# A two-part transformer kernel: its state-space layer's tables by closed form, its angles on GpSimd, its corrections on VectorE

## The chip, the cores and the metric

The kernel runs on one core of one Trainium2 chip. The metric is the device time of one launch, in microseconds (us). TensorE is called PE, VectorE DVE, ScalarE ACT, GpSimd POOL and SyncE SP, as in the profile; SP issues all transfers.

## What is computed

Two blocks of two layers each over 512 tokens of width 1024: a diagonal state-space layer (S5), sliding-window attention, MLPs, then a second block with a Mamba-2 layer and differential attention. Only the S5 layer, which comes first, is touched. For 64 groups of 16 channels with 64 complex states each:

```
dt = exp(log_dt);  a = exp(lam_re*dt) * (cos(lam_im*dt) + i sin(lam_im*dt))
coef = (a - 1) / lam;  bb = coef * b
x[t] = a * x[t-1] + bb @ u[t];   y[t] = Re(c @ x[t]) + d * u[t],  u = rmsnorm(h) * gain
mix = A * sigmoid(G),  (A, G) = gelu(y) @ w_glu
```

## The kernel before

**Tiling.** Tokens are cut into 64 steps of 8 (STEP), the groups into 8 blocks of 8 (GB). Within a step the recurrence is a small matrix product; from step to step it is a scan with the eighth power of a. The complex rotation is taken out of the scan, so that it has a real factor: the step sums are multiplied with cos and sin of angles (psi times the step's index) ahead of it and turned back behind it.

**The start.** s5_loads (L378) issues all loads on SP in one row: par, h, const, B, C, the first inputs Ur, then four units of weights. s5_vector (L492) forms dt's products, reduces the angle (L510), gets mag, sin and cos of one power from ACT (L430 to L433), and builds all powers of a by repeated complex products cmul (L546, six linked instructions each, eight calls, L564 to L572): TA for the outputs, PB for the inputs. Then signs (L593 to L595), the diagonal DI (L597), the first input tables (L600) and the step-wise norm factor ru (L603 to L606). link waits for each instruction before the next. Meanwhile ACT squares h in eight tiles through two buffers (L438) and PE sums them (L657).

**The loop.** Each engine runs step(T) for T = 0 to 9, on several blocks q at once. For block q = T: DVE's phases (L583: ang, k, f) give the fraction of a turn, ACT makes sinb and cosb (L448 to L452), scales the inputs by a gain in eight instructions (L456), POOL multiplies them by ru (L420) and forms the output tables TC by two products and a sum (L414 to L416), DVE the input tables TB (L579 to L581). PE transposes TB (L684, kept by ACT as ST, L461), forms the direct kernel K = TB x TC (L691, kept as Ksb, L465; DVE adds DI to its first part, Kd, L633), and the step sums S (L698, kept as Sx, L468). SP writes Ksb into Tm by eight transfers per block (L397). For q = T-1: PE turns Sx (JS, L667), DVE forms pr1, pr2, V, the scans Z and po1 (L617 to L626), PE turns Zb (JZ, L704), DVE forms po2 and W (L628, L630), and PE the outputs Y (L715, L716), kept by ACT as Ysb (L482). For q = T-2: PE transposes Ysb (YT, L675), ACT takes gelu twice (x1h at L475, a full one at L476) and DVE the remainder of the output, x1l (lo, L640).

**Order.** It is written out by hand: each engine's queue runs in program order, and Steps counters let one engine wait for a named operation of another. PE's order in step(T) is JS(T-1), YT(T-2), ST, K and S of T, JZ(T-1), Y(T-1). DVE's is pr1 to W of T-1, Kd(T), phases(T+1), tables(T+1), lo(T-2). Then glu_tensor (L757) runs 16 weight units of 24 matmuls (pe_unit, L173), and the rest of the kernel follows. The weights of units 0 to 2 are split by ACT ahead of the loop (L441) and by DVE there (L647).

Of the kernel before, what the change touches and what calls it, by code (L numbers as in the profile page):

```python
# [15 lines left out]
STEP = 8  # L16
# [26 lines left out]
PC, NPARAM = columns(PARAMS)  # L43

# [47 lines left out]
def program(nc, a):  # L92
    ctx = ExitStack()
    with ctx:
# [65 lines left out]
        par_loaded, h_loaded, const_loaded, bc_loaded = (sem(n) for n in ("par_loaded", "h_loaded", "const_loaded", "bc_loaded"))  # L160
# [12 lines left out]
        def pe_unit(e, u0, j, n4, xh, xl, first=None):  # L173
# [5 lines left out]
            for k in range(KT):  # L179
# [5 lines left out]
            last.then_inc(unit_done, 1)  # L185
# [99 lines left out]
        def own_buf(name, shape, dt=F32, lanes=LANES):  # L285
# [12 lines left out]
        PB = own_buf("PB", [2, SG, STEP])  # L298
# [14 lines left out]
                 "dt lrdt th k phi aphi k8 phi8 mag sn cs den rden nr c1 c2 t3 cr ci s2r s2i s4r s4i".split()}  # L313
        AR = own_buf("AR", [2, SG, STEP])
        cmA = own_buf("cmA", [SG, STEP])
        cmB = own_buf("cmB", [SG, STEP])
# [12 lines left out]
        assert at[0] <= x0_at + 32768  # L329
        grid = lambda t: t[:, :].rearrange("p (g c) -> p g c", g=GB)  # L330
        ang, kk, ff, absf = grid(bank[6]), grid(sq), grid(sd), grid(t32)

        zeroed, dt_ready, phase_ready, trig_ready, tables_ready, ru_ready = (
            sem(n) for n in ("zeroed", "dt_ready", "phase_ready", "trig_ready", "tables_ready", "ru_ready"))
# [43 lines left out]
        def s5_loads(e):  # L378
            e.dma_start(par[:, :], a["par"]).then_inc(par_loaded, 16)
            e.dma_start(h[:, :, :], a["xT"].rearrange("(k p) n -> p k n", p=LANES)).then_inc(h_loaded, 16)  # L380
            e.dma_start(const[:, :], a["const"]).then_inc(const_loaded, 16)
            e.dma_start(B_st[:, :, :, :], a["B"]).then_inc(bc_loaded, 16)
            e.dma_start(C_st[:, :, :, :], a["C"]).then_inc(bc_loaded, 16)
            e.dma_start(Ur[:, :, :], a["xu"][:, 0:GB]).then_inc(u_loaded, 16)

        def s5_sync(e):
# [3 lines left out]
            for q in range(NBLK):  # L390
                if q + 1 < NBLK:
                    e.wait_ge(s5_gained.sem, s5_gained.at("U1", q))
# [3 lines left out]
                for s in range(STEP):  # L396
                    e.dma_start(Tm[s * SH:(s + 1) * SH, q % 2, :, s:STEP, :],  # L397
                                Ksb[:, q % 2, :, 0:STEP - s, :]).then_inc(t_loaded[q % 2], 16)

        def s5_pool(e):  # L400
            e.memset(Tm[:, :, :, :, :], 0.0).then_inc(zeroed, 1)
            s5_pooled.open(e)
            e.wait_ge(h_loaded, 16)
            e.sem_inc(h_ready, 8)
            e.wait_ge(const_loaded, 16)
            e.wait_ge(bc_loaded, 32)
            e.wait_ge(tables_ready, 1)
            full = [LANES, GB, NSTEP]
            f4 = [LANES, GB, STEP + 1, SH]
            tt = e.tensor_tensor  # L410
            for q in range(NBLK):
                t, z = q, q % 2
                e.wait_ge(s5_out.sem, s5_out.at("Y2", q - 3))
                s5_pooled.took("TC1", tt(TC[:, q % 3], cut(C_st[:, 0], q).unsqueeze(2).to_broadcast(f4), cut(TA[:, 0], q).unsqueeze(3).to_broadcast(f4), ALU.mult))  # L414
                s5_pooled.next(e, t).took("TC2", tt(TCt[:, :, :, :], cut(C_st[:, 1], q).unsqueeze(2).to_broadcast(f4), cut(TA[:, 1], q).unsqueeze(3).to_broadcast(f4), ALU.mult))
                s5_pooled.next(e, t).took("TC", tt(TC[:, q % 3], TC[:, q % 3], TCt[:, :, :, :], ALU.add))  # L416
                if q == 0:
                    e.wait_ge(ru_ready, 1)
                e.wait_ge(s5_gained.sem, s5_gained.at("U1", q))
                s5_pooled.took("U", tt(Ub[:, z], Ub[:, z], ru[:, :].unsqueeze(1).to_broadcast(full), ALU.mult))  # L420
            e.wait_ge(s5_phases.sem, s5_phases.at("f", NBLK - 1))
# [3 lines left out]
        def s5_scalar(e):  # L425
            s = small
            e.wait_ge(par_loaded, 16)
            e.activation(s["dt"][:, :], V("log_dt"), ACT.Exp).then_inc(dt_ready, 1)
            e.wait_ge(phase_ready, 1)
            e.activation(s["mag"][:, :], s["lrdt"][:, :], ACT.Exp)  # L430
            e.activation(mag8[:, :], s["lrdt"][:, :], ACT.Exp, scale=8.0)
            e.activation(s["sn"][:, :], s["phi"][:, :], ACT.Sin)
            e.activation(s["cs"][:, :], s["aphi"][:, :], ACT.Sin, bias=half_pi[:, :], scale=-1.0).then_inc(trig_ready, 1)  # L433
            e.wait_ge(h_loaded, 16)
            for m in range(KT):
                if m >= 2:
                    e.wait_ge(acc_ready, m - 1)
                e.activation((sq if m % 2 else acc)[:, :], h[:, m], ACT.Square).then_inc(squared, 1)  # L438
            act_norm(e, 0, eps6)
            for v in range(3):  # L440
                act_split(e, v, 0)  # L441

            def step(T):
                if 0 <= T < NBLK:
                    q, t, z = T, T, T % 2
                    e.wait_ge(s5_phases.sem, s5_phases.at("f", t))
                    e.wait_ge(s5_angles.sem, s5_angles.at("cos", q - 1))
                    s5_angles.took("absf", e.activation(absf, ff, ACT.Abs))  # L448
                    e.wait_ge(s5_states.sem, s5_states.at("po2", q - 2))
                    s5_angles.took("sin", e.activation(sinb[:, z], ff, ACT.Sin, scale=SIN_SCALE))  # L450
                    e.wait_ge(s5_angles.sem, s5_angles.at("absf", t))
                    s5_angles.took("cos", e.activation(cosb[:, z], absf, ACT.Sin, bias=half_pi[:, :], scale=-SIN_SCALE))  # L452
                    e.wait_ge(u_loaded, 16 * q + 16)
                    e.wait_ge(s5_out.sem, s5_out.at("Y2", q - 2))
                    for g in range(GB):
                        last = e.activation(Ub[:, z, g], Ur[:, g], ACT.Copy, scale=V("gain_u", q * GB + g, q * GB + g + 1))  # L456
                    s5_gained.took("U1", last)
                    e.wait_ge(s5_sums.sem, s5_sums.at("S", q - 1))
                    for k in (1, 2):
# [2024 lines left out]
```

## Time and profile before

| what | value |
|---|---|
| median of 3 runs | 2131.9 us (2124.48 to 2132.26) |
| the profiled execution | 2129.69 us, its span 2127.8 us |
| PE busy | 1954.5 us (92%) |
| DVE busy | 1294.3 us (61%) |
| ACT busy | 912.3 us (43%) |
| POOL busy | 404.3 us (19%) |

The span runs from the first to the last instruction. In the 40 slices of the page (53 us each) PE is busy 2, 6, 7 and 8 tenths in the first four, which hold the S5 layer, and nearly full thereafter. The chain of work that ended last is 76% PE and 11% DVE.

### The profile page before, as it was taken

The numbers are of one execution on the slowest core, as the hardware profiler recorded it, in microseconds if no ns is written. First come the engines' busy times: TensorE is split into PE (matmuls) and PEld (weight loads), VectorE is DVE, ScalarE is ACT, GpSimd is POOL, SyncE is SP. The second block draws the span as 40 slices with busy tenths as digits, with TensorE's granted clock in tenths as the row PEclk, the third lists the DMA queues.
The fourth block names the chain that finished last, engine by engine and source line by source line (L and its number), as shares of the span: only waits on it lengthen the run. The fifth ranks groups of instructions, "written<-read, shape, count | busy, mean of one in ns | idle before, by whom it ended". The sixth has DMA issues, their size and how long they took to land.

```text
span 2127.8 us, 27339 instructions
## 1 busy us (share of the span) xinstructions
PE 1954.5 (92%) x9494; PEld 1570.0 (74%) x9494; DVE 1294.3 (61%) x1819; ACT 912.3 (43%) x1566; POOL 404.3 (19%) x275
## 2 busy tenths in 40 slices
PE   2678999999999976999999999999999998999996
PEld 1456878888888754778888887878878886777774
DVE  8884444434348779443433449887657765787763
ACT  2574442323234436342323334445535553456661
POOL 2650210000035010300000045152212223100003
PEclk7799999999999989999999999999999999999998
DMA  4111333333333210233333332212222222222211
GB/s 160 37 32 53 97 93 95 99 99 97 92 98 99 79 40 1 63 95 98 91 97 99 99 94 85 79 60 70 70 71 69 70 70 64 85 70 60 70 62 68
DMA packets 54088, 166.45 MB, mean 78 GB/s; under 512 B 13168, under 2 KB 13168, under 8 KB 53488
## 3 DMA queue, kind: packets, MB, share of 16 engines
q1 hardware_dynamic: 54000, 165.28, 25.3%
q8 instruction: 55, 0.90, 0.2%
q14 instruction: 33, 0.27, 0.0%
HBM read 160.80 MB, written 2.10 MB: 77 GB/s over the span
## 4 chain that ended last, share of the span: by engine, by line
PE 76%; DVE 11%; ACT 5%; POOL 3%; issue 3%; DMA 2%; DVEq 0%; POOLq 0%; SPq 0%; PEldq 0%; ACTq 0%
PE bank L182 15%; PE bank L184 15%; PE bank L183 15%; PE bank L1373 4%; PE bank L1375 4%; PE bank L1374 4%; DMA raw<-in_w_dram 2%; PE bank L1979 2%; PE bank L1981 2%; PE bank L1980 2%; POOL acc L232 1%; PE bank L1388 1%; PE bank L1389 1%; PE bank L1390 1%; DVE Sm L1141 1%
## 5 line engine op out<-in xcount | busy, mean ns | idle before, releaser
L201 DVE TENSOR_TENSOR w_lo<-raw,w_hi 128x1024 fp32r<-128x1024 f32 x289 | 369.3, 1279 | 463.8 <-ACT w_hi L193 462.3
L193 ACT ACTIVATE w_hi<-raw 128x1024 fp32r<-128x1024 f32 x289 | 305.6, 1058 | 631.6 <-DMA raw<-in_w_dram 631.5
L182 PE MATMUL bank<-x1h,w_hi 128*128 128x512 f32 x744 | 291.6, 392 | 6.5 <-DVE x1l L216 6.5
L184 PE MATMUL bank<-x1h,w_lo 128*128 128x512 f32 x744 | 290.2, 390 | 0.0
L183 PE MATMUL bank<-x1l,w_hi 128*128 128x512 f32 x744 | 290.1, 390 | 0.0
L182 PE MATMUL bank<-x0h,w_hi 128*128 128x512 f32 x704 | 278.3, 395 | 0.0
L184 PE MATMUL bank<-x0h,w_lo 128*128 128x512 f32 x704 | 274.5, 390 | 0.0
L183 PE MATMUL bank<-x0l,w_hi 128*128 128x512 f32 x704 | 274.4, 390 | 0.0
L230 POOL TENSOR_TENSOR sq<-h 128x512 f32 (+1 forms) x64 | 78.8, 1231 | 814.2 <-DVEq L812 659.3
L182 PEld LDWEIGHTS bank<-x1h,w_hi 128*128 128x128 f32 x744 | 139.8, 188 | 37.3 <-DVE x1l L216 7.8
L183 PEld LDWEIGHTS bank<-x1l,w_hi 128*128 128x128 f32 x744 | 139.9, 188 | 29.3 <-issue 0.5
L184 PEld LDWEIGHTS bank<-x1h,w_lo 128*128 128x128 f32 x744 | 139.9, 188 | 29.0
L1373 PE MATMUL bank<-x1h,w_hi 128*128 128x512 f32 x384 | 156.6, 408 | 0.0
L182 PEld LDWEIGHTS bank<-x0h,w_hi 128*128 128x128 f32 x704 | 132.2, 188 | 29.5 <-issue 2.2
L183 PEld LDWEIGHTS bank<-x0l,w_hi 128*128 128x128 f32 x704 | 132.2, 188 | 29.5 <-issue 2.3
L184 PEld LDWEIGHTS bank<-x0h,w_lo 128*128 128x128 f32 x704 | 132.2, 188 | 27.4
L1374 PE MATMUL bank<-x1l,w_hi 128*128 128x512 f32 x384 | 151.8, 395 | 0.0
L1375 PE MATMUL bank<-x1h,w_lo 128*128 128x512 f32 x384 | 151.8, 395 | 0.0
L232 POOL TENSOR_TENSOR acc<-acc,sq 128x512 f32<-128x512 f32 x64 | 103.5, 1617 | 5.0
L791 DVE TENSOR_TENSOR x1l<-a,x1h 128x512 f32 x64 | 44.3, 693 | 92.7 <-ACT a L781 92.7
L779 ACT ACTIVATE x1h<-t 128x512 f32 x64 | 40.5, 632 | 132.1 <-DVE t L789 132.1
L1373 PEld LDWEIGHTS bank<-x1h,w_hi 128*128 128x128 f32 x384 | 73.5, 191 | 17.9 <-issue 1.9
(410 smaller groups left out, 3476.6 us busy)
## 6 DMA issues: line engine op xcount, KB each, us to landing
raw<-in_w_dram SPq DMA_DIRECT2D x289, 512.0 KB, 3.6
h<-in_xT_dram SPq DMA_DIRECT2D x1, 2048.0 KB, 9.0
Ur<-in_xu_dram SPq DMA_DIRECT2D x8, 256.0 KB, 2.7
out_dram<-h SPq DMA_DIRECT2D x8, 256.0 KB, 2.1
const<-in_const_dram SPq DMA_DIRECT2D x1, 1425.0 KB, 11.9
B_st<-in_B_dram SPq DMA_DIRECT2D x1, 1024.0 KB, 13.8
C_st<-in_C_dram SPq DMA_DIRECT2D x1, 1024.0 KB, 16.2
p_in<-in_pT_dram SPq DMA_DIRECT2D x1, 1024.0 KB, 4.8
```

What stands on the lines that cost most here:

```text
L182: e.matmul(b, w_hi[:, w, k], xh[:, k], start=(k == 0), stop=False)
L183: e.matmul(b, w_hi[:, w, k], xl[:, k], start=False, stop=False)
L184: last = e.matmul(b, w_lo[:, w, k], xh[:, k], start=False, stop=(k == KT - 1))
L193: e.activation(w_hi[:, z], raw[:, z], ACT.Copy).then_inc(hi_split, 1)
L201: e.tensor_tensor(w_lo[:, z], raw[:, z], w_hi[:, z].bitcast(F32), ALU.subtract).then_inc(w_split, 1)
L230: e.tensor_tensor(one(sq[:, :]), tile(h, m), tile(h, m), ALU.mult).then_inc(squared, 1)
L232: e.tensor_tensor(acc[:, :], acc[:, :], sq[:, :], ALU.add).then_inc(acc_ready, 1)
L791: e.tensor_tensor(tile(x1l, m), one(a32[:, :]), tile(x1h, m).bitcast(F32), ALU.subtract).then_inc(a_ready, 1)
L1373: e.matmul(b, w_hi[:, w, k], x1h[:, k], start=(k == 0), stop=False)
L1374: e.matmul(b, w_hi[:, w, k], x1l[:, k], start=False, stop=False)
L1375: last = e.matmul(b, w_lo[:, w, k], x1h[:, k], start=False, stop=(k == KT - 1))
L1979: e.matmul(b, w_hi[:, w, k], xh[:, k], start=(k == 0), stop=False)
```

## The change

- **Powers in closed form.** cmul, its eight calls, the sign passes and AR go. mag, sin and cos of all nine powers (128x576) come from ACT at once, and DVE multiplies them to PB. The gain goes into B (block 0 by DVE, the rest by POOL in two products) from a new input, and into the diagonal. The tables of block 0 are formed before the coefficient, which goes into C's powers: c_powers, six products for block 0's groups, then six for the others.
- **Loads.** par and const come in two parts, the S5 layer's first; a row of gains (512 KB) is added ahead of B. B and C have semaphores of their own.
- **Angles.** ang, k and f are formed by POOL (f lies in R, not in sd), as is U, now one product from Ur without ACT's eight (U(0) by DVE).
- **VectorE** adds DI straight from the bank in two halves (K, Kd), so ACT keeps one part of eight less; lo moves between po2 and W of the next step; the split of units 0 to 2 moves into the loop's step 7 (ACT's to steps 3 to 5).
- **PE** begins step(T) with ST and K of T, JS follows Y, and six of eight k-tiles of GLU's unit 0 are multiplied in step 8, ahead of Y(7). Squares have four buffers.

```diff
         def s5_loads(e):
-            e.dma_start(par[:, :], a["par"]).then_inc(par_loaded, 16)
+            e.dma_start(par[:, 0:S5_PARAM], a["par"][:, 0:S5_PARAM]).then_inc(par_loaded, 16)
             e.dma_start(h[:, :, :], a["xT"].rearrange("(k p) n -> p k n", p=LANES)).then_inc(h_loaded, 16)
-            e.dma_start(const[:, :], a["const"]).then_inc(const_loaded, 16)
+            e.dma_start(const[:, 0:S5_CONST], a["const"][:, 0:S5_CONST]).then_inc(const_loaded, 16)
+            e.dma_start(gain_row[:, :, :], a["gain"].rearrange("p (g h) -> p g h", g=SG)).then_inc(g_loaded, 16)
...
         def s5_pool(e):
+            for part in range(2):
+                e.tensor_tensor(B_st[:, part, GB:], B_st[:, part, GB:], gain_row[:, GB:], ALU.mult).then_inc(b_gained, 1)
...
+            def inputs(q):
+                e.wait_ge(u_loaded, 16 * q + 16)
+                e.wait_ge(s5_out.sem, s5_out.at("Y2", q - 2))
+                s5_inputs.took("U", tt(Ub[:, q % 2], Ur[:, :, :], ru[:, :].unsqueeze(1).to_broadcast(full), ALU.mult))
+
+            def angles(q):
+                e.wait_ge(s5_angles.sem, s5_angles.at("sin", q - 1))
+                s5_phases.took("ang", tt(ff, cut(psi, q).unsqueeze(2).to_broadcast(full), C("cidx").unsqueeze(1).to_broadcast(full), ALU.mult))
+                s5_phases.next(e, q).took("k", e.tensor_scalar(kk, ff, ROUND, ROUND, ALU.add, ALU.subtract))
+                s5_phases.next(e, q).took("f", tt(ff, ff, kk, ALU.subtract))
+
+            e.wait_ge(tables_ready, 1)
+            angles(0)
+            tables(0)
+            e.wait_ge(tables_ready, 2)
+            for T in range(NBLK + 2):
+                if 0 <= T + 1 < NBLK:
+                    tables(T + 1)
...
+                    angles(T + 1)
...
+                    inputs(T + 1)
...
         def s5_vector(e):
...
+            tt(power["mag"][:, :, :], over(v("lrdt")), sidx, ALU.mult).then_inc(magnitudes, 1)
...
+            link(e, stt(PB[:, 1], mag, V("sgn"), power["sin"][:, :, :], ALU.mult, ALU.mult))
...
+            link(e, tt(PB[:, 0], mag, power["cos"][:, :, :], ALU.mult))
...
+            tables(0)
...
+            c_powers(0, GB)
...
+            s5_inputs.took("U", tt(Ub[:, 0], Ur[:, :, :], ru[:, :].unsqueeze(1).to_broadcast(full), ALU.mult))
+            c_powers(GB, SG)
...
+            def direct(T):
+                for k in (1, 2):
+                    e.wait_ge(s5_k_kept.sem, s5_k_kept.at(f"K{k}", T))
+                    s5_direct.took("K" if k == 1 else "Kd", tt(Ksb[:, T % 2, 4 * k - 4:4 * k, 0, :], kbank(k)[:, :, 0, :], DI[:, T * GB + 4 * k - 4:T * GB + 4 * k], ALU.add))
...
+                if 1 <= T < NBLK:
+                    direct(T)
+                if 0 <= q < NBLK:
                     e.wait_ge(s5_out.sem, s5_out.at("JZ", t))
                     s5_states.took("po2", tt(turned, turned, sinb[:, z], ALU.mult))
                     e.wait_ge(s5_out.sem, s5_out.at("Y2", q - 1))
+                    if q:
+                        low(q - 1)
                     n().took("W", tt(Wb[:, :, 1:], tA[:, :, :NSTEP - 1], turned[:, :, :NSTEP - 1], ALU.add))
...
                 if 0 <= T + 1 < NBLK:
-                    phases(T + 1)
                     tables(T + 1)
...
         def s5_tensor(e):
...
+                if 0 < T < NBLK:
+                    step_sums(T)
...
+                    if T == NBLK:
+                        pe_unit(e, U_GLU, 0, 0, x1h, x1l, lambda k: (x_ready, k + 1), range(0, 6))
                     e.wait_ge(s5_states.sem, s5_states.at("W", t))
...
+                if 0 < T < NBLK:
+                    rotated(T)
```

## Rows read from the trace of the kernel before

**Rows 1.** Stretches: length, busy PE, PEld, DVE, ACT, POOL; granted clock, DMA share, GB/s.

```profile
0.00:77.72 77.72, 26.46 (x100) 15.60 (x100) 62.27 (x127) 27.66 (x53) 31.53 (x16) 0.74 0.33 120
77.72:176.15 98.43, 71.14 (x510) 53.55 (x510) 81.71 (x133) 69.13 (x130) 44.59 (x22) 0.91 0.15 32
176.15:186.32 10.17, 6.31 (x45) 4.41 (x45) 6.97 (x17) 3.85 (x6) 0.00 (x0) 0.95 0.17 29
186.32:199.50 13.18, 12.44 (x65) 11.19 (x66) 3.39 (x3) 5.20 (x6) 0.00 (x0) 0.78 0.01 2
199.50:2127.80 1928.30, 1838.18 (x8775) 1485.20 (x8773) 1139.92 (x1543) 806.41 (x1372) 328.18 (x237) 0.98 0.26 80
```

**Rows 2.** Chain that ended last, start of the kernel: start us, us, what.

```profile
37.08 1.22 DVE TB L579
...
44.46 3.04 DVE ru L603
```

**Rows 3.** The same chain through one block of the loop.

```profile
99.13 0.84 PE bank L675 x9
...
101.87 2.14 PE bank L691 x15
...
107.70 0.68 DVE Wb L630
...
111.11 1.13 DVE TB L579
...
114.63 1.01 DVE x1l L640
...
115.77 0.84 PE bank L675 x9
```

**Rows 4.** Timeline, 61 to 68 us: start us, us, engine, line; first POOL, then DVE.

```profile
62.50 3.48 POOL L416 TENSOR_TENSOR TC<-TC,TCt 128x1152 f32<-128x1152 f32 x1
...
61.85 1.64 DVE L579 TENSOR_TENSOR TB<-B_st,PB 128x1024 f32<-128x1024 f32 x1
63.42 3.63 DVE L580 TENSOR_TENSOR TBt<-B_st,PB 128x1024 f32<-128x1024 f32 x1
```

**Rows 5.** Timeline of POOL in a later block.

```profile
134.10 1.27 POOL L420 TENSOR_TENSOR Ub<-Ub,ru 128x512 f32<-128x512 f32 x1 [8.03 <-ACT Ub L456]
135.33 2.14 POOL L414 TENSOR_TENSOR TC<-C_st,TA 128x1152 f32<-128x1152 f32 x1
...
140.10 2.63 POOL L416 TENSOR_TENSOR TC<-TC,TCt 128x1152 f32<-128x1152 f32 x1
```

**Rows 6.** DMA issues of the first 40 us: KB, us from issue to landing.

```profile
B_st<-in_B_dram SPq DMA_DIRECT2D x1, 1024.0 KB, 13.8
```

**Rows 7.** Timeline: small DVE product, scans, JS, Tm's issues, ACT's gelu, GLU's first matmul.

```profile
18.33 0.28 DVE L551 TENSOR_TENSOR cmB<-s_s4i 128x64 f32<-128x64 f32 x1
...
182.09 1.53 DVE L624 TENSOR_TENSOR_SCAN Zb<-mag,bank 128x64 f32<-128x64 f32 x8
...
111.69 1.13 PE L667 MATMUL bank<-Sx,const 128*128 128x512 f32 x2
...
77.94 5.08 SPq L397 DMA_DIRECT2D Tm<-Ksb  x8
...
174.36 1.28 ACT L475 ACT_TABLE_LOAD   x1
175.66 1.10 ACT L475 ACTIVATE x1h<-bank 128x512 fp32r<-128x512 f32 x1
...
193.94 0.50 PE L182 MATMUL bank<-x1h,w_hi 128*128 128x512 f32 x1
```

**Rows 8.** Groups of instructions by line: POOL's forms nearest to the moved ones.

```profile
L232 POOL TENSOR_TENSOR acc<-acc,sq 128x512 f32<-128x512 f32 x64 | 103.5, 1617 | 5.0
...
L2227 POOL TENSOR_TENSOR ol<-OT,oh 128x512 fp32r<-128x512 f32 x8 | 10.4, 1302 | 252.4 <-ACT oh L2179 252.4
...
L1088 POOL COPY Ks<-kdup 128x512 f32 x4 | 2.4, 612 | 10.7 <-PE bank L1106 5.3 <-DVE q L982 5.0 <-POOL Vs L1091 0.4
```

More of the change, by code:

```diff
@@ L178, in pe_unit @@
             e.wait_ge(bank_free, after(u0, j, n4, 1))
-            for k in range(KT):
+            for k in ks:
                 if first is not None:
@@ L312, in program @@
         small = {n: own_buf("s5_" + n, [SG]) for n in
[L313 to L316, printed above, removed]
+                 "dt lrdt th k phi den t3 g1 g2 nr c1 c2 c3 w ci dg".split()}
+        power = {n: own_buf("s5_" + n, [SG, STEP + 1]) for n in "turns whole mag sin cos".split()}
+        cm = [own_buf(f"cm{i}", [SG, STEP + 1]) for i in range(4)]
         ru3 = own_buf("ru3", [NSTEP, STEP])
@@ L411, in s5_pool, with tables @@
-            for q in range(NBLK):
-                t, z = q, q % 2
+            def tables(q):
                 e.wait_ge(s5_out.sem, s5_out.at("Y2", q - 3))
                 s5_pooled.took("TC1", tt(TC[:, q % 3], cut(C_st[:, 0], q).unsqueeze(2).to_broadcast(f4), cut(TA[:, 0], q).unsqueeze(3).to_broadcast(f4), ALU.mult))
[L415 to L420, printed above, removed]
@@ L449, in step @@
[L449 to L456, printed above, removed]
@@ new lines, in s5_vector @@
+            link(e, stt(v("phi"), v("k"), -TWO_PI_HI, v("th"), ALU.mult, ALU.add))
+            link(e, stt(v("phi"), v("k"), -TWO_PI_LO, v("phi"), ALU.mult, ALU.add))
+            turns, whole, mag = (power[n][:, :, :] for n in ("turns", "whole", "mag"))
+            link(e, stt(turns, over(v("phi")), 1.0 / (2 * math.pi), sidx, ALU.mult, ALU.mult))
+            link(e, ts(whole, turns, ROUND, ROUND, ALU.add, ALU.subtract))
+            link(e, tt(turns, turns, whole, ALU.subtract))
+            e.sem_inc(power_steps, 1)
@@ new lines, in direct @@
+            def direct(q):
+                e.wait_ge(s5_pooled.sem, s5_pooled.at("TC", q))
+                e.wait_ge(s5_direct.sem, s5_direct.at("Kd", q - 1))
+                for k in (1, 2):
+                    e.wait_ge(s5_k_kept.sem, s5_k_kept.at(f"K{k}", q - 1))
+                    for g in range(4):
+                        gg = 4 * k - 4 + g
+                        last = e.matmul(bank[5][64 * (k - 1):64 * (k - 1) + SH, g * LANES:(g + 1) * LANES], TB[:, gg, 0], TC[:, q % 3, gg, 0:STEP].rearrange("p s h -> p (s h)"), start=True, stop=True)
+                    s5_k.took(f"K{k}", last)
@@ new lines, in step_sums @@
+            def step_sums(q):
+                e.wait_ge(s5_inputs.sem, s5_inputs.at("U", q))
+                e.wait_ge(s5_st_kept.sem, s5_st_kept.at("ST2", q))
+                e.wait_ge(s5_kept.sem, s5_kept.at("Sx", q - 1))
+                e.wait_ge(s5_states.sem, s5_states.at("pr1", q - 1))
+                for g in range(GB):
+                    last = e.matmul(bank[2][:, g * NSTEP:(g + 1) * NSTEP], ST[:, g], Ub[:, q % 2, g], start=True, stop=True)
+                s5_sums.took("S", last)
@@ L2445, in lay_out @@
     v["log_dt"] = over(ssm_log_dt[0])
+    v["sidx"] = over(np.arange(9, dtype=f))
+    v["sgn"] = np.where(np.arange(128) < 64, -1, 1).astype(f)[:, None]
+    v["nsgn"] = -v["sgn"]
     v["gain_u"] = np.tile(norm_mix[0].reshape(64, 16).T, (8, 1))
@@ L2478 @@
     a = {n: nc.dram_tensor(f"in_{n}_dram", arrays[f"in_{n}_dram"].shape, F32, kind="ExternalInput").ap()
-         for n in ("w", "const", "par", "xT", "xu", "B", "C", "pT")}
+         for n in ("w", "const", "par", "xT", "xu", "gain", "B", "C", "pT")}
     a["out"] = nc.dram_tensor("out_dram", (DM, TOK), F32, kind="ExternalOutput").ap()
```

392 lines of the change are left out of this document (203 added, 189 removed).

## Prediction

> **What bounds the kernel now.** The page's slices come first: PE is nearly full from the fourth slice on, so only the S5 layer has air in it, and what lies behind that layer is untouched. The stretches [rows 1] say how much: 199.5 us pass until GLU's first unit is done, with PE busy 116 of them, and then come 1928.3 us with PE busy 1838. What the first 199.5 us save, the rest starts earlier by: the weights of GLU's fifth unit are fetched when its first unit ends, now as after, and the units between are loaded by then. So I count three parts: the start, up to the end of W(0) (77.72); six intervals from W(0) to W(6) (98.43, so 16.4 each); and the end (10.17 to W(7), 13.18 to the end of unit 0).
>
> The chain of waits tells who sets each part. In the start it is DVE: its linked power section lasts until 37.08, then come the first tables and, from 44.46, the factor ru [rows 2]. In the loop [rows 3] a block goes YT, transposes, K, S and JZ on PE up to 107, then po2, W, Kd, phases, tables and lo on DVE up to 115.6, then YT again, 16.64 after the last. DVE waits for PE and PE for DVE, half the time each. POOL is busy 44.6 of 98.4 us there [rows 1] and bounds nothing.
>
> One thing more must be seen, because the change leans on POOL. Its sum TC, queued at 62.50, takes 3.48 [rows 4], and 2.63 in a later block [rows 5]. A table product of DVE was running until 61.85 + 1.64 = 63.49; 2.63 more is 66.12, close to where POOL ends, 65.98. DVE's next product, queued at 63.42, takes 3.63 and ends at 67.05: POOL's end plus 1.07, where such a product alone takes 1.13 [rows 3, 4]. So an operation of POOL and one of DVE that both read two tensors of SBUF do not overlap at all: each waits out the other's whole instruction.
>
> The Trainium skill says the same (SBUF — State Buffer, section "SBUF: two separate sides"): the port pair is locked for a whole instruction, whoever starts first, and not shared. It speaks against moving work to POOL, and the trace agrees. Were the ports shared without a lock, the sum would be rival 1's, 2100.
>
> **The change, part by part: the start.** The 33 us of linked DVE work go. In their place, ahead of the first tables, stand some twenty DVE operations. A line through 128x64 (0.28 [rows 7]) and 128x1024 (1.13 [rows 3]) gives 0.75 for 128x576 and 0.67 for 504 columns; a dozen small and seven of 576, with ACT's load of the sine table (1.28, as gelu's [rows 7]), make 9 to 10 us behind par's landing near 4: 13 to 14. Then B decides. It landed 13.8 behind its issue [rows 6] at 2.3, so at 16.1, with 5.1 MB in front of and in it. By the column counts par and const shrink by 0.3 and 1.1 MB and the gain row adds 0.5: 0.9 MB less, at 5.1 MB in 13.8 us 2.4, at the rate without the first transfer's own delay about 2.1. I take 14.0, between 13 (power section) and 16.1 (nothing gained). Then:
> - B's gain on DVE 0.4, three tables at 1.15, and locked between them POOL's two gain products of 128x896. The line through U (512, 1.27) and TC's first product (1152, 2.14) [rows 5] gives 1.79 each. With gaps 7.5: 21.5.
> - Nine operations at 0.27 and six of c_powers at 0.31: 4.3. TA of block 0 is there at 25.8. The norm on PE is done by about 21 and in nobody's way.
> - POOL's ang, k, f and its three TC operations, 10.4 with gaps (priced below), and four DVE operations locked between them (ru's product, U(0), two of c_powers, 0.67 each): TC(0) at 38.9. K takes 2.1 to 2.7 on PE.
> - DVE ends c_powers at 41.5, waits for POOL's next product (43.8), and forms DI, 1.2: 45.0. tables(1), three at 1.15, wait for 2.14, 2.63 and 1.15 of POOL: 54.4.
> - K and Kd 0.6; pr1, pr2, V at 0.68 and Z at 1.53 [rows 7], 3.6; po1 behind POOL 2.0; K, Kd, po2 and W 2.1: W(0) ends at 62.7.
>
> That is 15.0 us ahead of 77.72. Tm's eight transfers for block 0 are issued from 55.0 on, in 5 to 6 us [rows 7], and land just at W(0): 0 to 1 us, taken as 0.
>
> **The loop.** DVE loses phases (2.1 a block, on the chain: 108.97 to 111.11 is their place ahead of the tables [rows 3]). ACT loses eight gains a block, beside other work, worth nothing; its cover is that Sx now comes behind gelu and before Y. POOL gains ang, k and f, none of which the trace shows there. ang: two spread operands like U, bounds 1.0 and 1.27, I take 1.15. k reads one tensor: between the copy of 128x512, 0.61, and U's 1.27, I take 0.70, the copy being nearest. f: two dense tensors, 1.30 or 1.62 [rows 8]; I take 1.27, as U. POOL then does 2.14 + 2.14 + 2.63 + 1.15 + 0.70 + 1.27 + 1.27 = 11.3, with seven gaps of 0.07 11.8. DVE's three tables and po1 add 3 x 1.15 + 0.67 = 4.1 in which POOL stands: **15.9 a block**. Operations that read a bank do not count (W took 0.68 in each block), and K and Kd now read one.
>
> The chain of PE and DVE without POOL would be: W's end to JS 3.3 [rows 3, 7], JS 1.1, transposes 1.5, K 2.4, its keeping 0.5, gelu's table 1.3, gelu twice 1.7, lo 1.0, W 0.7, gaps 0.4: **13.9**. With POOL in the way the tables wait twice or thrice and end some 7.5 behind W, not 3.5; transposes, K, YT, gelu, lo and W then take 8.8. That is **16.3**. The two limits, 15.9 and 16.3, lie together; I take 16.3. Six blocks give 97.8 against 98.43. So what phases gave back is spent on waits for POOL. Gain 0.6.
>
> **The end.** From W(6) to W(7) the three splits hide behind Y(6) and JS(7), and lo(6), 1.0, now stands ahead of W(7): 11.2 against 10.17, a loss of 1.0. From W(7): 18 early GLU matmuls, 0.23 each (24 from 193.94 [rows 7] to 199.5), 4.1, begin behind JZ(7) and end 1.7 behind W(7). Then Y 3.3, keeping 0.6, YT 0.9, gelu 1.7, lo 1.0 and the last six matmuls 0.9 with gaps: 10.3 against 13.18. Gain 2.9. The granted clock averaged 0.78 there [rows 1]; at 1.2 GHz the early matmuls would take 4 more.
>
> **Sum.** 15.0 + 0.6 - 1.0 + 2.9 = 17.5 us. The profiled execution, 2129.69 (its span, 2127.8, and 1.9 around it), becomes 2112.2. The median of the runs is 2.2 above that execution: 2114.
>
> **Rivals.**
> 1. **POOL is not in the way.** Its operations fall where DVE waits for PE. A block goes at the chain's 13.9, six save 14 more: 2100. For: DVE still waits several us a block. Against: POOL would be busy 11.8 of 13.9, and DVE wants 4.1 of that lock. Chance 0.13.
> 2. **POOL is dearer.** k 1.27, f 1.62, ang 1.27: 1.04 more a block, over seven blocks 7.3, and B as late as before, 2.1: up to 2124, 2121 if only one holds. Chance 0.20.
> 3. **Slower: each table operation waits for a whole TC operation.** If the loop settles so that tables(T+1) always meet POOL's three TC operations, they cost 3.5 + 6.9; with 8.8 for the rest and 1.3 for po1 that is 20.5 a block. Six blocks lose 25 on 16.4, the rest still gains 17: 2140. It decides from 19.2 a block on, where the gain is eaten. For: three tables took 7.4 in just this way from 37.08 on [rows 2]. Against: POOL needs 15.9 of 20.5 and could not be there each time. Chance 0.06.
> 4. The change does not do what it says, the new parts lying off the path: 2131. Chance 0.01.
>
> **The numbers.** Forecast 0.60, rivals 0.13, 0.20, 0.06, 0.01. About 0.5% (10.7 us) is what a measurement of this kernel can tell from no change. Faster: the forecast, rival 1 and half of rival 2, 0.83. Within: the other half and rival 4, 0.11. Slower: 0.06. The range goes from rival 1's 2100, less 2 for a start with fewer locks, to rival 2's 2124.
>
> **What would show it.** The first tables begin near 14 and W(0) ends near 63. POOL is busy almost without a break from 26 to 150 us, with ang, k and f at 1.15, 0.70 and 1.27. The three tables of a block take 6 to 8 us, not 3.5; W to W is near 16.3; unit 0 ends near 182. I am wrong if W(0) ends later than 70, if W to W is under 15 or over 18, or if the time behind unit 0 is not 1928 within 4 us.

## The result, and the profile of the changed kernel

| | kernel before | changed kernel |
|---|---|---|
| median of the runs, us | 2132.1 (4 runs, 2124.5 to 2132.6) | 2101.2 (4 runs, 2100.1 to 2104.1) |
| profiled execution, us | 2129.69 (span 2127.8) | 2101.99 (span 2100.2) |

The ratio is 0.9873, 95% interval 0.9844 to 0.9901: 31 us faster between the medians, 27.6 between the profiled spans. The forecast was 2114, 17.5 us faster, with a range of 2098 to 2124. The sign and the range held; the size did not.

The stretches of the changed kernel, cut as in [rows 1] (length; busy PE, PEld, DVE, ACT, POOL; granted clock, DMA share, GB/s):

```profile
0.00:62.39 62.39, 27.30 (x100) 16.31 (x100) 53.36 (x78) 19.81 (x29) 39.81 (x23) 0.73 0.43 157
62.39:153.04 90.65, 74.16 (x512) 60.00 (x511) 83.96 (x121) 62.30 (x89) 80.77 (x41) 0.87 0.17 38
153.04:165.74 12.70, 10.36 (x52) 8.21 (x53) 9.99 (x19) 5.91 (x8) 0.00 (x0) 0.77 0.04 7
165.74:178.25 12.51, 9.74 (x60) 7.82 (x60) 1.85 (x5) 5.20 (x6) 0.00 (x0) 0.91 0.01 1
178.25:2100.20 1921.95, 1835.10 (x8775) 1481.52 (x8773) 1144.74 (x1544) 806.86 (x1372) 326.58 (x237) 0.98 0.27 80
```

| part | before | forecast | measured | gain forecast | gain measured |
|---|---|---|---|---|---|
| start to W(0) | 77.72 | 62.7 | 62.39 | 15.0 | 15.3 |
| W(0) to W(6) | 98.43 | 97.8 | 90.65 | 0.6 | 7.8 |
| W(6) to W(7) | 10.17 | 11.2 | 12.70 | -1.0 | -2.5 |
| W(7) to the end of unit 0 | 13.18 | 10.3 | 12.51 | 2.9 | 0.7 |
| behind unit 0 | 1928.30 | 1928.3 | 1921.95 | 0 | 6.3 |

So three things need an explanation: the loop gains 7.2 us more than forecast, the end 3.7 less, and 6.3 us come from a part that no edit touches.

In the steady blocks of the loop, the third to the fifth, both engines are now full. DVE's timeline through one block, from a W to the next:

```profile
93.44 0.68 DVE L687 TENSOR_TENSOR Wb<-tA,bank 128x504 f32<-128x504 f32 x1 [0.16 <-DVE x1l L602]
94.03 2.82 DVE L594 TENSOR_TENSOR TB<-B_st,PB 128x1024 f32<-128x1024 f32 x1
96.78 2.06 DVE L595 TENSOR_TENSOR TBt<-B_st,PB 128x1024 f32<-128x1024 f32 x1
98.87 1.51 DVE L596 TENSOR_TENSOR TB<-TB,TBt 128x1024 f32<-128x1024 f32 x1
...
103.92 1.95 DVE L678 TENSOR_TENSOR tA<-Zb,cosb 128x512 f32<-128x512 f32 x1
...
106.28 0.70 DVE L683 TENSOR_TENSOR bank<-bank,sinb 128x512 f32<-128x512 f32 x1
106.89 1.08 DVE L602 TENSOR_TENSOR x1l<-bank,x1h 128x512 fp32r<-128x512 f32 x1
108.13 0.68 DVE L687 TENSOR_TENSOR Wb<-tA,bank 128x504 f32<-128x504 f32 x1 [0.16 <-DVE x1l L602]
```

and POOL's, which has no idle time in it but gaps of up to 0.09 between operations:

```profile
93.15 2.62 POOL L432 TENSOR_TENSOR TC<-TC,TCt 128x1152 f32<-128x1152 f32 x1
95.74 2.02 POOL L441 TENSOR_TENSOR R<-psi,const 128x512 f32<-128x512 f32 x1
97.84 2.78 POOL L442 TENSOR_SCALAR sq<-R 128x512 f32<-128x512 f32 x1
100.70 1.27 POOL L443 TENSOR_TENSOR R<-R,sq 128x512 f32<-128x512 f32 x1
101.94 1.28 POOL L437 TENSOR_TENSOR Ub<-Ur,ru 128x512 f32<-128x512 f32 x1
103.17 2.16 POOL L430 TENSOR_TENSOR TC<-C_st,TA 128x1152 f32<-128x1152 f32 x1
105.40 2.47 POOL L431 TENSOR_TENSOR TCt<-C_st,TA 128x1152 f32<-128x1152 f32 x1
107.96 2.62 POOL L432 TENSOR_TENSOR TC<-TC,TCt 128x1152 f32<-128x1152 f32 x1
```

The first table operation (TB, L594) ends 1.09 after POOL's TC: it waited for all of TC, as in [rows 4]. The second waits for ang in the same way. The third does not wait for k: it runs at 98.87 to 100.38, inside k's 97.84 to 100.62, and takes 1.51, 0.3 more than alone. That is what the forecast had otherwise.

One wait has gone. In the kernel before, DVE sat idle at po2 until PE had turned Zb (JZ), in all six blocks, 13.6 us in all; this is one of them:

```profile
123.54 0.70 DVE L628 TENSOR_TENSOR bank<-bank,sinb 128x512 f32<-128x512 f32 x1 [2.17 <-PE bank L704]
```

In the changed kernel po2 (L683, above) follows at once, and this wait is 1.0 us in all six blocks. PE's order differs in one point that the list of the change does not name: JZ(T-1) now stands ahead of the step sums S of T and not behind them. DVE's time without work falls from 16.7 us to 6.7 over the six blocks, while its busy time, waits for POOL included, rises from 81.7 to 84.0.

In the experiments below, "W to W" is the time from the end of one block's W to that of the next, and its mean is from W(0) to W(6): 16.4 before, 15.1 in the changed kernel (16.3 and 15.4 for the first two blocks, then 14.6 to 14.8).

### The profile page after: what moved, and what is told of

It is laid out like the page before. It is cut to its first block, busy times and chain, and to the rows that moved or that the text cites. A ratio compares the mean times of both kernels' runs of the same rounds, so it can differ in the third digit from the quotient of the medians.

```text
span 2100.2 us, 27247 instructions
## 1 busy us (share of the span) xinstructions
PE 1956.6 (93%) x9494; PEld 1573.9 (75%) x9494; DVE 1293.9 (62%) x1762; ACT 900.1 (43%) x1503; POOL 447.2 (21%) x300
## 4 chain that ended last, share of the span: by engine, by line
PE 75%; DVE 11%; ACT 5%; issue 3%; POOL 3%; DMA 2%; DVEq 0%; POOLq 0%; SPq 0%; ACTq 0%; PEldq 0%
PE bank L183 15%; PE bank L185 15%; PE bank L184 15%; PE bank L1448 4%; PE bank L1450 3%; PE bank L1449 3%; PE bank L2054 2%; DMA raw<-in_w_dram 2%; PE bank L2056 2%; PE bank L2055 2%; PE bank L1463 1%; POOL acc L234 1%; PE bank L1464 1%; PE bank L1465 1%; ACT w_hi L195 1%
## 6 DMA issues: line engine op xcount, KB each, us to landing
const<-in_const_dram SPq DMA_DIRECT2D x1, 1028.0 KB, 15.7
B_st<-in_B_dram SPq DMA_DIRECT2D x1, 1024.0 KB, 11.5
C_st<-in_C_dram SPq DMA_DIRECT2D x1, 1024.0 KB, 13.2
```

## The experiments

**Does POOL have room, and is the move worth anything?** Each expectation says what its theories A and B are; the letters do not stand for the same thing in all of them.

E1 gives the angles back to DVE, all else as changed (the first lines are POOL's, the others DVE's; phases forms ang in a bank, k and f, as in the kernel before):

```diff
-                if 0 <= T + 1 < NBLK:
-                    angles(T + 1)
...
                 if 0 <= T + 1 < NBLK:
+                    phases(T + 1)
                     tables(T + 1)
```

> The changed kernel with one part undone: ang, k and f of each block are formed by VectorE ahead of its tables again. Theory A (GpSimd's queue sets the block: 12.5 us of its own work and 2.3 us of waits for VectorE's tables make the 14.8 that stand between two W): with the three gone GpSimd needs some 8.2 plus waits and falls idle, the chain of PE and VectorE takes over with 2.1 us more on it, and W to W becomes 16 to 16.7; six intervals lose 7 to 11 us, the time is 2108 to 2113. Theory B (moving the angles was worth nothing, since VectorE's waits for GpSimd give it back, as forecast; the gain in the loop came from the new order of lo, ST and K): W to W stays 14.5 to 15.2, the time within 3 us of 2101.

Measured: 2105.1 us (4 runs, 2102.9 to 2108.2), ratio 0.9888 (0.9862 to 0.9915). W to W is 14.9 on the mean, no longer than with POOL's angles: theory B, though the time is 3.9 us above the changed kernel's and not within 3. W(0) ends at 66.2 instead of 62.4. The tables take 1.22 each again, for POOL is out of the way, and DVE's queue is full with its own work:

```profile
97.48 0.69 DVE L591 TENSOR_TENSOR bank<-psi,const 128x512 f32<-128x512 f32 x1
98.21 0.69 DVE L592 TENSOR_SCALAR sq<-bank 128x512 f32<-128x512 f32 x1
99.01 0.69 DVE L594 TENSOR_TENSOR R<-bank,sq 128x512 f32<-128x512 f32 x1
99.62 1.22 DVE L584 TENSOR_TENSOR TB<-B_st,PB 128x1024 f32<-128x1024 f32 x1
```

What follows: moving the angles to POOL is worth nothing in the loop. Taking 2.1 us off DVE bought 2.2 us more of waits for POOL. Its gain, 3.8 us, is in the start, where DVE's queue decides; the times of the whole runs alone do not show it, for the intervals of the ratios overlap. The shorter loop came from the rest of the change. In E1 too the wait for JZ is gone (0.9 us in all), which points at PE's new order; no run puts that order back by itself.

E2 lets POOL form k twice; E3 leaves k out (its f multiplies by zeros, so the rotation angles are left out).

```diff
# E2
+                s5_phases.next(e, q).took("j", e.tensor_scalar(kk, ff, ROUND, ROUND, ALU.add, ALU.subtract))
                 s5_phases.next(e, q).took("k", e.tensor_scalar(kk, ff, ROUND, ROUND, ALU.add, ALU.subtract))
# E3
-                s5_phases.next(e, q).took("k", e.tensor_scalar(kk, ff, ROUND, ROUND, ALU.add, ALU.subtract))
-                s5_phases.next(e, q).took("f", tt(ff, ff, kk, ALU.subtract))
+                s5_phases.next(e, q).took("f", tt(ff, ff, kk, ALU.mult))
```

> The changed kernel with GpSimd's rounding k done twice in each block (same values). Theory A: GpSimd's queue is full, so each block gets the whole cost, 1.9 us (k alone took 1.92 at 83.90): W to W 16.5 to 16.8, six intervals 10 to 12 us longer. Theory B (the chain of PE and VectorE sets the block): GpSimd has room, W to W grows by less than 0.5.

> The changed kernel without the rounding k; f multiplies the angle by a tile of zeros instead, so all sines and cosines are those of angle zero. It leaves out the rotation's angles. Theory A: GpSimd's demand falls to some 10.6 plus waits of 3.4, about 14.0, where the chain of PE and VectorE (13.9 by the sum of rows) takes over: W to W 13.9 to 14.3. Theory B: no change from 14.8 within 0.3. A third outcome, 14.5 to 14.8 with GpSimd idle, would say that VectorE's third table product, which now ran beside k, waits for a whole operation instead.

Measured, one run each: E2 2120.2 us, W to W 17.2 on the mean, 2.1 more than in the profiled execution of the changed kernel; E3 2100.0 us, W to W 14.7, 0.4 less. E2's pair, POOL's timeline:

```profile
105.26 2.78 POOL L442 TENSOR_SCALAR sq<-R 128x512 f32<-128x512 f32 x1
108.12 1.92 POOL L443 TENSOR_SCALAR sq<-R 128x512 f32<-128x512 f32 x1
```

and E3's third table operation, POOL's line first:

```profile
108.05 2.13 POOL L444 TENSOR_TENSOR R<-R,sq 128x512 f32<-128x512 f32 x1
109.08 2.18 DVE L598 TENSOR_TENSOR TB<-TB,TBt 128x1024 f32<-128x1024 f32 x1
```

What follows: with an operation of 1.92 us more, POOL is idle in no block of E2, and a block is longer by 2.1 on the mean, or by 1.4 against the longer pattern shown below (15.8). So POOL has no room. Taken away, k brings 0.4 (1.1 against the longer pattern), and POOL is idle 1.4 to 3.0 us in each of the first five blocks. That is the third outcome that E3's expectation names: DVE's third table operation, which ran beside k in the changed kernel, now waits out f and takes 2.18 instead of 1.51. (The mean is B's number too, but B has no such wait.) What k gave back is in part spent on a wait for a two-input operation.

**How much of it repeats?** E4 is the changed kernel again, E8 the kernel before again, E12 the changed kernel once more, timed against seven runs of the kernel before.

> The changed kernel once more, unedited, for the time behind GLU's first unit. Behind that unit the profiled execution took 6 us less than before the change (1922 against 1928), which no edit explains. If it is chance from run to run, this run lies anywhere in 1919 to 1930 there; if it hangs on the shift of the start or on the units' first order, it is 1922 within 1 again.

> The kernel before, unchanged, once more. Its profiled time behind unit 0 was 1928.3 us, the changed kernel's 1922.0 though no edit touches that part. Theory A (chance): this run shows other values in the attention stretch (220.5 in the one, 218.2 to 219.8 in the changed ones), the Mamba stretch (518.2 against 514.6 to 515.5) and the differential attention (298.6 against 297.0 or 300.3), and the part behind unit 0 takes 1922 to 1926. Theory B (the change does something there): 1928 again, with 518.2 and 220.5. Loop: 16.4 a block in both.

> The changed kernel, unchanged, timed in as many rounds as the two variants with ACT's angles, whose ratios to the kernel before were 0.985 (0.9827 to 0.9872) and 0.9848 (0.983 to 0.9865). Theory A (the variants gain what their shorter blocks say, 2 to 5 us): the ratio is 0.987 to 0.989. Theory B (their lead is chance between runs): 0.985 to 0.986. The profiled loop shows 14.8 or 15.75 a block, or a mixture of both patterns.

E4 took 2108.7 us. Its loop settled in another order: W to W 15.75 on the mean. Behind unit 0 it had 1925.3 us, so not the 1922 again. E12's profiled loop did as E4's (15.8), with the medians at 2102.8 (4 runs, 2101.3 to 2104.3) against 2127.9, ratio 0.9876 (0.9860 to 0.9893), within its theory A. The timeline in E12, DVE's and then POOL's TC:

```profile
108.48 2.04 DVE L594 TENSOR_TENSOR TB<-B_st,PB 128x1024 f32<-128x1024 f32 x1
110.44 3.64 DVE L595 TENSOR_TENSOR TBt<-B_st,PB 128x1024 f32<-128x1024 f32 x1
114.12 1.95 DVE L596 TENSOR_TENSOR TB<-TB,TBt 128x1024 f32<-128x1024 f32 x1
...
109.52 3.48 POOL L432 TENSOR_TENSOR TC<-TC,TCt 128x1152 f32<-128x1152 f32 x1
```

Here the tables start 1.0 us ahead of POOL's TC, where in the other pattern they start 0.9 behind its start. So TCt, the whole of TC (3.48) and then ang pass between them. They end 7.5 us behind W instead of 6.3: the 7.5 of the forecast, with W to W half a microsecond under its 16.3. The same code has both patterns, 1 us a block apart. E5, E7 and E11 below leave the loop's code as it is: W to W is 15.1 in E5 and E11, and 15.6 in E7.

E8 took 2129.7 us. Its W to W is 16.65 on the mean, 0.25 more than in the first execution, where its expectation had 16.4 in both. The end of its first unit, read from the ACT operation behind it, was at 201.8, later than the 199.5 of the profiled execution of before, and the rest took less, 1926.0, the upper end of theory A:

```profile
0.00:201.80 201.80, 118.61 (x720) 86.75 (x721) 154.84 (x276) 105.83 (x194) 76.08 (x38) 0.81 0.21 64
201.80:2127.80 1926.00, 1836.52 (x8776) 1483.24 (x8774) 1140.02 (x1543) 807.96 (x1372) 328.77 (x237) 0.98 0.26 80
```

From GLU's first sigmoid to the end of the span, the two executions of before have 1926.7 and 1924.3 us, the changed kernel's three 1920.5, 1923.9 and 1920.4; the other kernels, alike in that part, 1917.4 to 1929.8. The mean of the two is 1925.5, that of all eleven changed ones (E7 apart, which has work behind its end) 1923.1. The pieces that move are the attention stretch (218 to 223 us in all executions), the Mamba stretch (518.2 in before's first execution, 515.0 in its second, 512 to 517 in the others) and the differential attention, which took 297.0 to 297.2, 298.6, or 299.9 to 300.3, whatever the kernel. What follows: most of the 6.3 us behind unit 0 is chance of one execution; whether the 2.4 between the means is more than that is open. Why these stretches have several lengths was not tried.

**What does a POOL operation take from DVE?** E7 puts single operations behind the finished kernel, 128x512 f32 in SBUF; the last line is DVE's, the others POOL's.

```diff
+            ts2 = lambda: e.tensor_scalar(sq[:, :], acc[:, :], ROUND, ROUND, ALU.add, ALU.subtract)
+            two = lambda: e.tensor_tensor(sq[:, :], acc[:, :], R[:, :], ALU.mult)
...
+            two = lambda: e.tensor_tensor(a32[:, :], t32[:, :], sd[:, :], ALU.mult)
```

> The changed kernel whole, and behind it single operations on 128x512 f32 in SBUF: on POOL add-and-subtract with one tensor input twice, a single add twice, a two-input product twice; then three add-and-subtract of POOL against eight two-input products of DVE; then three two-input products of POOL against six of DVE. Alone, add-and-subtract is expected at 1.92 as k in the loop, the product at 1.27 as U, DVE's product at 0.67. Theory A (forecast: any POOL operation on SBUF locks): each of POOL's three add-and-subtracts takes one DVE product out for its whole 1.92, so a DVE product beside it takes 0.67 to 2.6. Theory B (one-input operations of POOL do not lock): DVE's eight products go at 0.7 to 1.0 each beside them, while in the second pairing they take up to 1.27 + 0.67 = 1.94.

Alone, the add-and-subtract took 1.92, one single add 1.49, the product 1.26, DVE's product 0.69. Together, in order of time, first the one-input operations of POOL with DVE's products:

```profile
2113.42 2.35 POOL L2317 TENSOR_SCALAR sq<-acc 128x512 f32<-128x512 f32 x1 [1.61 <-DVE a L2342]
2114.02 0.98 DVE L2342 TENSOR_TENSOR a<-t,sd 128x512 f32<-128x512 f32 x1
2115.04 0.69 DVE L2342 TENSOR_TENSOR a<-t,sd 128x512 f32<-128x512 f32 x1
2115.76 0.69 DVE L2342 TENSOR_TENSOR a<-t,sd 128x512 f32<-128x512 f32 x1
2115.86 2.38 POOL L2317 TENSOR_SCALAR sq<-acc 128x512 f32<-128x512 f32 x1
2116.49 0.98 DVE L2342 TENSOR_TENSOR a<-t,sd 128x512 f32<-128x512 f32 x1
```

then the two-input ones:

```profile
2122.77 1.59 POOL L2319 TENSOR_TENSOR sq<-acc,R 128x512 f32<-128x512 f32 x1
2123.28 1.63 DVE L2342 TENSOR_TENSOR a<-t,sd 128x512 f32<-128x512 f32 x1
2124.44 1.59 POOL L2319 TENSOR_TENSOR sq<-acc,R 128x512 f32<-128x512 f32 x1
2124.94 1.63 DVE L2342 TENSOR_TENSOR a<-t,sd 128x512 f32<-128x512 f32 x1
```

Against a two-input operation each DVE product takes 1.63, 0.94 more than alone. The pairs follow each other 1.67 apart, where the two operations alone take 1.26 and 0.69, so of 1.95 us all but 0.3 is one after the other; "each waits out the whole instruction" is right but for these 0.3. Against k's kind one product in three is longer, by 0.29, and two run at full speed while POOL is in its 1.92; POOL's own operation grows by 0.43 to 0.46, where a product of DVE ran on for 0.57 to 0.60 behind its start. So by these rows k waits for a product of DVE that is running when k starts, holds DVE back for 0.29, and overlaps with the rest. That is theory B, and the 1.51 of the third table beside k says the same in the kernel. The Trainium skill (SBUF — State Buffer, section "SBUF: two separate sides"), as the prediction read it, has the port pair locked for a whole instruction; the two-input pairs here agree but for the 0.3, k does not.

**The order of lo, and the early part of GLU.** E6 puts lo(T-2) back behind the tables, E5 makes GLU's first unit whole again.

```diff
# E6
-                    if q:
-                        low(q - 1)
...
-                if T == NBLK + 1:
+                if 0 <= T - 2 < NBLK:
                     low(T - 2)
# E5
-                    if T == NBLK:
-                        pe_unit(e, U_GLU, 0, 0, x1h, x1l, lambda k: (x_ready, k + 1), range(0, 6))
```

> The changed kernel with lo(T-2) back behind the tables, as before the change; nothing is left out. Theory A (the chain of PE and DVE sets the block): lo leaves the way to W, W falls 1.1 us sooner behind gelu, and W to W goes to about 13.9. Theory B (DVE's queue is full): lo costs the same 1.08 wherever it stands, W to W stays between the 14.8 and 15.75 us that two runs of the changed kernel showed. Theory C: the early place is what shortened the loop; then W to W is above 16. Time: A 2095, B 2099 to 2109, C above 2110.

> The changed kernel with GLU's first unit whole again behind the last lo; nothing is left out. Read from the end of W(7) to the end of unit 0 (12.5 us in the changed kernel), since the loop ahead of it may settle differently. Theory A (forecast's term): the early 18 matmuls hide behind W(7) but for 1.7 us and save 4.1 - 1.7 = 2.4 us at 0.23 a matmul, so the stretch grows by 2.4 or more, to 15 or more; if the late ones run at the 0.43 pace that the changed kernel's last six show, to 20. Theory B: the early matmuls ran at the low clock and held Y(7) back by 3.0 us, so what they save is spent: Y(7) starts 3 us sooner, 24 matmuls at 0.23 take 5.5, and the stretch stays at 12 to 13.

E6: 2104.9 us (4 runs, 2103.4 to 2112.2), ratio 0.9902 (0.9885 to 0.9918); W to W 15.5 on the mean, 15.6 in its steady blocks. DVE's queue is nearly as full (0.3 us idle a block), and the tables take TBt 3.64 and TB 1.95, the longer pattern. So lo costs its time wherever it stands in a full queue: theory B. Whether its late place favours the longer pattern, one profiled execution can't tell, as the changed kernel has that pattern too.

E5: 2103.0 us. From the end of W(7) to the end of unit 0 it took 13.2 us, to the first sigmoid 14.6; the changed kernel took 12.5 and 13.9, the kernel before 13.2 and 14.8. So the early part is worth 0.7, where the forecast's terms for it give 2.4. PE's timeline in the changed kernel shows where it went:

```profile
163.82 0.63 PE L185 MATMUL bank<-x1h,w_lo 128*128 128x512 f32 x1
164.25 0.63 PE L183 MATMUL bank<-x1h,w_hi 128*128 128x512 f32 x1
...
168.19 0.39 PE L184 MATMUL bank<-x1l,w_hi 128*128 128x512 f32 x1
168.41 0.39 PE L185 MATMUL bank<-x1h,w_lo 128*128 128x512 f32 x1
168.73 0.43 PE L783 MATMUL bank<-Tm,Ub 128*64 128x128 f32 x2
```

The early matmuls start 0.43 us apart, nearly twice the 0.23 of later: PE works at 1.2 GHz there (granted clock 0.64 from 162 to 165), behind a JZ for which it had waited 2.3 us. By 166.4 it is back at 2.4 GHz. Y(7) stands behind them and starts 3.0 behind W(7), not 1.7. Theory B, but for 0.7.

Three other kernels tell what the full clock gives. In E3, E10 and E11 PE waited the same 2.3 us for JZ(7), yet the early matmuls ran at the full clock throughout. E11's:

```profile
159.60 0.40 PE L185 MATMUL bank<-x1h,w_lo 128*128 128x512 f32 x1
159.84 0.40 PE L183 MATMUL bank<-x1h,w_hi 128*128 128x512 f32 x1
...
163.36 0.43 PE L780 MATMUL bank<-Tm,Ub 128*64 128x128 f32 x2
```

Y(7) starts 1.4 behind W(7) in all three, and unit 0 ends 10.9 behind it, 2.3 less than in E5: the price of the forecast, at the clock that it took. So the wait alone does not bring the low clock; what does is not shown.

**What sets the start?** E11, used above for its end, leaves out POOL's two gain products, and with them the gain on B's columns of blocks 1 to 7.

```diff
-            for part in range(2):
-                e.tensor_tensor(B_st[:, part, GB:], B_st[:, part, GB:], gain_row[:, GB:], ALU.mult).then_inc(b_gained, 1)
```

> The changed kernel without POOL's two gain products of B; left out is the gain on B's columns for blocks 1 to 7. Theory A (forecast: DVE's first tables wait out both products, 1.8 each): tables(0) end 3.6 us sooner, at 17.2 instead of 20.8 where B lands alike, c_powers and POOL's start of ang follow, and W(0) ends at 58.8. Theory B (something else, the norm or par, then decides): tables(0) sooner, W(0) within 1 of 62.4.

DVE's timeline in E11, to set beside 2.98, 3.10 and 1.22 in the changed kernel:

```profile
14.92 1.22 DVE L592 TENSOR_TENSOR TB<-B_st,PB 128x1024 f32<-128x1024 f32 x1
16.06 1.22 DVE L593 TENSOR_TENSOR TBt<-B_st,PB 128x1024 f32<-128x1024 f32 x1
17.32 1.23 DVE L594 TENSOR_TENSOR TB<-TB,TBt 128x1024 f32<-128x1024 f32 x1
```

The first tables end at 18.5 instead of 22.0, and W(0) at 58.3 instead of 62.4. Theory A: the gains' lock is 3.5 of the start, and it goes through to W(0) undiminished (4.1, or 3.7 against the 62.0 of E4 and E12). (The whole run, 2100.7 us, gained nothing by it: behind the first sigmoid it had 1924.6, among the longer values.)

**A version with less locked work.** E9 has ACT form the angle product of blocks 1 to 7; E10 also keeps the cosine in a free bank.

```diff
# E9
-                s5_phases.took("ang", tt(ff, cut(psi, q).unsqueeze(2).to_broadcast(full), C("cidx").unsqueeze(1).to_broadcast(full), ALU.mult))
...
+                if 0 <= T + 1 < NBLK:
+                    e.wait_ge(s5_angles.sem, s5_angles.at("sin", T))
+                    for g in range(GB):
+                        e.activation(ff[:, g], C("cidx"), ACT.Copy, scale=psi[:, (T + 1) * GB + g:(T + 1) * GB + g + 1]).then_inc(ang_done, 1)
# E10, on top of it
+        cosb = bank[6][:, :].rearrange("p (z g c) -> p z g c", z=1, g=GB)
...
-                    s5_states.took("pr1", tt(tA[:, :, :], grid(bank[2]), cosb[:, z], ALU.mult))
+                    s5_states.took("pr1", tt(tA[:, :, :], Sx[:, z], cosb[:, 0], ALU.mult))
```

> The changed kernel with the angle products of blocks 1 to 7 formed by ACT, eight one-input scalings of 128x64 a block behind its cosine; POOL keeps k and f. Nothing is left out. Theory A (the lock is the bound): in a block POOL's two-input operations take 9.4 us, DVE's three table operations and po1 4.3, and no two of them overlap, 13.7 of the 14.8; without the angle product 12.5 remain, and W to W goes to 13.4 to 13.9, six blocks save 5 to 8 us: 2093 to 2096. Theory B (the queues' order sets the block, or ACT, busy 11 of 14.8 and now 13, becomes the bound): W to W stays at 14.6 or more, 2100 or later.

> As the run before, and the cosine table goes to a free bank instead of SBUF, so that po1 reads one tensor of SBUF; pr1 takes the kept copy of the sums instead of the bank. Nothing is left out. Theory A (the lock is the bound): po1 no longer waits for POOL (0.7 instead of 1.95), the locked work of a block falls to 11.9, and POOL's own 11.3 with gaps 11.8 comes next: W to W 12.5 to 13.2, a further 4 us: 2089 to 2092. Theory B: po1 drops to 0.7 but another product waits instead, W to W as in the run before within 0.3.

E9: 2094.0 us (5 runs, 2091.3 to 2099.2), ratio 0.9850 (0.9827 to 0.9872), W to W 14.4. E10: 2095.0 us (5 runs, 2093.7 to 2099.3), ratio 0.9848 (0.9830 to 0.9865), W to W 14.2. Both are faster than both kernels by their medians, by 8 us against E12; their intervals overlap E12's 0.9860 to 0.9893 a little, so the lead is likely and not certain. E9's time falls into theory A's 2093 to 2096, but its 14.4 a block lies between A and B; behind the first sigmoid it had 1917.4, the shortest of all. In one of E9's later blocks DVE sits idle, where in the changed kernel's steady blocks it did not:

```profile
106.27 2.00 ACT L532 ACTIVATE R<-const,psi 128x64 f32<-128x64 f32 x8
...
108.43 2.01 POOL L448 TENSOR_SCALAR sq<-R 128x512 f32<-128x512 f32 x1 [1.99 <-ACT R L532]
...
111.99 0.70 DVE L681 TENSOR_TENSOR bank<-bank,sinb 128x512 f32<-128x512 f32 x1 [1.19 <-PE bank L757]
```

What follows: the locked work did bound the block in part. The expectation's sum for it, 9.4 + 4.3, leaves out one of POOL's six two-input operations: 2.14 + 2.14 + 2.63 + 1.09 + 1.27 + 1.26 is 10.5, and with DVE's 4.3 it is 14.9, against the 14.8 of a steady block of the changed kernel. In E9 the sum is 13.8. Four of its six blocks took 13.7 to 14.1, the other two 15.3 and 15.5. In three blocks DVE was idle for 1.1 to 2.3 us, for PE's JS and ACT's gelu. In E10 po1 takes 0.69 instead of 1.95, and the block shortens by 0.2: its theory B. DVE is idle there for 0.9 us or more in every block, mostly for ACT's gelu. So the chain of PE, ACT and DVE, 13.9 by the forecast's sum, may be next; no run shows that it bounds.

## Why the prediction was right, and where it was wrong

**The start** was right in nearly all of its steps. B was there at 14.3 (14.0 forecast; it landed 11.5 behind its issue, not 13.8). tables(0) ended at 22.0 (21.5), TA of block 0 at 26.1 (25.8), TC(0) at 39.1 (38.9), DI at 47.4 (45.0), tables(1) at 54.5 (54.4), W(0) at 62.4 (62.7). POOL's gain products fell between the tables as priced: TB took 2.98 in the start, 1.76 more than the 1.22 alone, where 1.79 stood. Three things inside were off and made up for each other: k took 2.24 instead of 0.70, DI met one product of POOL more than reckoned (3.18, and 2.4 later), and tables(1), one less (7.0 for the three instead of 9.4). That they did is luck.

**The loop** is the mis-sized term: 15.1 a block against 16.3, 7.2 us in all. The step that failed is the sentence that each operation waits out the other's whole instruction, applied to k, and with it "three tables and po1 add 4.1 in which POOL stands". k costs 1.92 and not 0.70, which makes POOL's own work 12.5 instead of 11.3. But the third table runs beside k, and the waits of POOL in a steady block sum to 0.9 for ang, 0.9 for k and 0.3 for TCt, 2.1 in place of 4.1. The two errors leave a smaller demand: 14.6, with gaps 14.8, which is the block as measured, where 15.9 stood. The other limit, 7.5 for the tables and 8.8 for the rest, was 6.3 and 8.4 in that execution. Its steady blocks lie just under the 15 that the prediction named as a sign of being wrong. The tables' part was 7.5 in E4 and E12, where W to W was 15.75 to 15.8: so about 4 of the 7.2 us are the pattern that the profiled execution happened to be in, and the other 3 the mis-sized terms. That neither phases nor POOL would give anything ("what phases gave back is spent on waits for POOL") was right, and E1 shows it. What did shorten the block, against 16.4 and 16.65 before, was then not the angles. E1, with the angles on DVE, no eight gains on ACT and the new order of K, S, JS, JZ and lo, has 14.9; the parts of this rest were not parted further, except lo, which has none. The traces show where it went, the wait for JZ at po2 (13.6 us over six blocks before, 1.0 after), and that this wait would end is not counted in the prediction.

**W(6) to W(7)** was forecast at 11.2 and took 12.7. In E12 it took 11.2. The difference is PE's clock: pairs of Y(6)'s matmuls started 0.43 us apart, with a granted clock of 0.66 from 152 to 157, in the one, and 0.22 apart with 1.00 in the other. The reckoning was right for a full clock and left out the low one, and the low one is the usual case: of the twelve executions of the changed kernel and its variants only E12 and E6 had the full clock there (11.2 and 11.3); nine took 12.7 to 13.0, and E2, which has more work, 15.7.

**The end** was forecast at 10.3 and took 12.5. The prediction named the price, "at 1.2 GHz the early matmuls would take 4 more", and did not take it: 8 of the 18 ran so. With all 18 at the full clock the stretch took 10.9 (E3, E10, E11), so 1.6 of the 2.2 is this term. Of the last six, the three behind the wait for lo also went at 0.43.

**Behind unit 0** the text said 1928 within 4 or it is wrong: it was 1922.0. E8 shows 1926 for the unchanged kernel and the others both more and less, so this was mostly chance in the measured span, and the bound of 4 was too tight for one execution. The four parts ahead of it sum to 21.3 us, against 17.5 forecast; the medians gave 31 in the first comparison and 25 in E12's. So the sum of the gain is nearer to the truth than its terms: the loop gave more than was said and the end less.

**The rivals.** Rival 1, POOL not in the way, gave the nearest time, 2100, but by a wrong mechanism: E2 refutes it, POOL has no room. Of rival 2's prices only k's came true, and more (1.92 for 1.27); f took 1.27, ang 1.09, and B was not late. Rival 3, tables meeting all three TC operations, does not occur; two of them meet in the longer pattern.

## What to carry to other kernels

Before moving work from DVE to POOL, sum for one turn of the loop the two-input SBUF operations of both engines, and the own work of each. Here the turn came out near the sum of the two-input operations (14.9 against 14.8), and never far under it (14.3 in E3, by what pairs overlap). What the move took off DVE came back as waits for POOL (E1). POOL's add-and-subtract with one input is slow, but it takes little from DVE, so it is the one to lay beside DVE's products (other one-input operations were not tried); giving the work to a third engine did better here, likely but not certainly (E9). Look first for a wait that a queue's order makes: here 13.6 us at one product of DVE. Where two full queues meet, the same code can settle in different patterns, here 1 us a block apart, so a loop is judged from several executions.

## What the runs showed of the hardware that was not expected

- An add-and-subtract of POOL on 128x512 f32, one input and one output, takes 1.92 us, half as much again as a two-input product of the same size (1.26); with one operation it takes 1.49. Per element it is dearer than the copy of the same size (0.61, [rows 8]) threefold.
- That operation and a two-input product of DVE overlap, but for 0.29 us that DVE loses near its start and up to 0.46 that POOL loses to a product already running (E7). Two two-input operations overlap by 0.3 of 1.95 us only.
- DVE's product of 16x64 (dg) took 2.19 beside POOL's first product of TC, where one of 128x64 takes 0.23 alone: it waited out the 2.14 of POOL's product like a large one.
